# A two-layer hybrid encoder trunk: adding the two scan directions of every head on VectorE

## The reference, cut to what matters

```python
def ssd_chunked(xs, dt, a, bm, cm):
    ...
    a_cs = jnp.cumsum((dt * a).reshape(b, c, t, g, e), axis=2)
    ...
    seg = a_cs[:, :, :, None] - a_cs[:, :, None, :]
    decay = jnp.exp(jnp.where(lower, seg, -jnp.inf))
    cb = jnp.einsum('bclgn,bcsgn->bclsg', Cc, Bc)
    y_diag = jnp.einsum('bclsge,bcsgep->bclgep', cb[..., None] * decay, X)
    ...
# called twice, and both results added: y = y_fwd + y_bwd + d_skip * xs
```

## Time and profile before

| | |
|---|---|
| time, median of 3 runs | 1656.96 us (1655.63 to 1657.75) |
| the profiled execution: time | 1656.37 us |
| its span on the core | 1654.6 us |
| PE busy | 1634.1 us, 99% of the span |
| DVE busy | 993.3 us, 60% |
| POOL busy | 674.2 us, 41% |
| granted TensorE clock | 1.0 of full speed |

### The profile page before, as it was taken

How to read it: one execution, slowest core, us unless ns; L and a number is a source line. 1 busy time by engine, 2 the same in 40 slices (tenths; PEclk the granted TensorE clock), 3 DMA queues, 4 the chain that set the end, 5 groups by cost and what they waited for, 6 DMA issues and landing times.

```text
span 1654.6 us, 20299 instructions
## 1 busy us (share of the span) xinstructions
PE 1634.1 (99%) x7864; PEld 1297.6 (78%) x7864; DVE 993.3 (60%) x1564; ACT 661.9 (40%) x916; POOL 674.2 (41%) x339
## 2 busy tenths in 40 slices
PE   7999999999999999999999999999999999999999
PEld 5777778877878888888877777787878788888887
DVE  4589869787764455522227898798887554554000
ACT  5455552335343333332244555523443433333221
POOL 3332222233445555554443222223244555555443
PEclk9999999999999999999999999999999999999999
DMA  5532135442222222222224221444522223222223
GB/s 170 139 91 74 60 117 146 134 146 94 90 90 99 93 91 100 89 92 96 92 90 127 87 74 62 124 146 130 149 95 90 90 89 100 92 91 98 95 92 109
DMA packets 57375, 170.93 MB, mean 103 GB/s; under 512 B 5984, under 2 KB 11872, under 8 KB 57280
## 3 DMA queue, kind: packets, MB, share of 16 engines
q1 hardware_dynamic: 56896, 168.88, 32.1%
q0 software_dynamic: 384, 0.75, 0.4%
HBM read 166.24 MB, written 3.38 MB: 103 GB/s over the span
## 4 chain that ended last, share of the span: by engine, by line
PE 92%; issue 2%; DVE 2%; POOL 1%; DMA 1%; ACT 1%; SPq 0%; DVEq 0%; POOLq 0%; ACTq 0%
PE banks L1158 27%; PE banks L1160 27%; PE banks L1159 27%; PE banks L1257 2%; PE banks L1236 2%; PE banks L1245 2%; PE banks L1322 1%; PE banks L1309 1%; PE banks L1336 1%; DMA sb_w_raw<-w_out 1%; PE banks L1216 1%; DVE sb_h_lo L809 0%; POOL sb_xc L473 0%; PE banks L1293 0%; DVE sb_squares L822 0%
## 5 line engine op out<-in xcount | busy, mean ns | idle before, releaser
L433 POOL TENSOR_TENSOR sb_w_lo<-sb_w_raw,sb_w_hi 128x1024 fp32r<-128x1024 f32 x200 | 482.4, 2412 | 634.9 <-ACT sb_w_hi L528 634.9
L1158 PE MATMUL banks<-sb_h_hi,sb_w_hi 128*128 128x512 f32 x1344 | 550.9, 410 | 11.3 <-POOL sb_w_lo L433 9.9
L528 ACT ACTIVATE sb_w_hi<-sb_w_raw 128x1024 fp32r<-128x1024 f32 x256 | 270.9, 1058 | 706.9 <-PE banks L1160 691.4
L1160 PE MATMUL banks<-sb_h_hi,sb_w_lo 128*128 128x512 f32 x1344 | 530.9, 395 | 0.0
L1159 PE MATMUL banks<-sb_h_lo,sb_w_hi 128*128 128x512 f32 x1344 | 530.6, 395 | 0.0
L1158 PEld LDWEIGHTS banks<-sb_h_hi,sb_w_hi 128*128 128x128 f32 x1344 | 253.5, 189 | 92.4 <-issue 34.7
L1159 PEld LDWEIGHTS banks<-sb_h_lo,sb_w_hi 128*128 128x128 f32 x1344 | 253.8, 189 | 60.9 <-issue 6.5
L1160 PEld LDWEIGHTS banks<-sb_h_hi,sb_w_lo 128*128 128x128 f32 x1344 | 253.5, 189 | 59.4
L1123 DVE TENSOR_TENSOR banks<-banks,sb_rstd 128x512 f32<-128x512 f32 x88 | 61.5, 699 | 145.3 <-PE banks L1160 135.7
L1160 PE MATMUL banks<-sb_ff_hi,sb_w_lo 128*128 128x512 f32 x352 | 138.9, 395 | 0.0
L1159 PE MATMUL banks<-sb_ff_lo,sb_w_hi 128*128 128x512 f32 x352 | 138.9, 395 | 0.0
(11 more groups left out here) (202 smaller groups left out, 2255.9 us busy)
## 6 DMA issues: line engine op xcount, KB each, us to landing
sb_w_raw<-w_in SPq DMA_DIRECT2D x88, 512.0 KB, 3.4
sb_w_raw<-w_up SPq DMA_DIRECT2D x88, 512.0 KB, 3.3
sb_w_raw<-w_out SPq DMA_DIRECT2D x32, 512.0 KB, 3.3
sb_w_raw<-w_down SPq DMA_DIRECT2D x32, 512.0 KB, 3.3
sb_e<-sum_rows SPq DMA_DIRECT2D x16, 512.0 KB, 6.2
sb_bias_t<-bias_rows SPq DMA_DIRECT2D x16, 448.0 KB, 5.6
sb_exp_cs<-sum_rows SPq DMA_DIRECT2D x32, 192.0 KB
sb_w_raw<-w_down SPq DMA_DIRECT2D x16, 384.0 KB, 3.0
```

The lines of the kernel that those rows point to most:

```text
L433: g.tensor_tensor(WLO[:, n % 2, :], W[:, n % 2, :], WHI[:, n % 2, :].bitcast(F32), ALU.subtract).then_inc(w_lo.handle, 1)
L528: sc.activation(WHI[:, n % 2, :], W[:, n % 2, :], ACT.Copy).then_inc(w_hi.handle, 1)
L1158: mm(out, whi, hhi, start=start, stop=False)
L1160: return mm(out, wlo, hhi, start=False, stop=stop)
```

## The change

It does four things. `seg` becomes one subtraction over both directions and all chunks (128x1024, the columns of AS broadcast along the row) and then one minimum with 80 in place, which waits for the subtraction. `add_directions` moves from POOL to DVE, and is done for every head, behind `low_after`. `within` multiplies the sums of both heads: 8 products instead of 12. And `within` waits for the sums of both heads (`gs_done`), no longer for `g_done`.

```diff
--- before.py
+++ after.py
@@ -276,7 +276,7 @@
     cb_mm, cb_done, xs_done, st_mm, sin_done = sem("cb_mm", 2), sem("cb_done", 4), sem("xs_done", 12), sem("st_mm", 12), sem("sin_done", 8)
     seg_done, e_done, g_done, y_mm = (
         sem(n, SSD_HEADS) for n in ("seg_done", "e_done", "g_done", "y_mm"))
-    gs_done = sem("gs_done", SSD_HEADS // 2)
+    gs_done = sem("gs_done", SSD_HEADS)
     yo_mm, y_read, t_read, z_copied, y_comb = (sem(n, 8) for n in ("yo_mm", "y_read", "t_read", "z_copied", "y_comb"))
     z_done = sem("z_done", 2)
     ff_tap, ff_silu, ff_hi, ff_lo = sem("ff_tap", 2 * FF_T), sem("ff_silu_done", FF_T), sem("ff_hi_done", FF_T), sem("ff_lo_done", FF_T)
@@ -458,11 +458,6 @@
             g.tensor_tensor(SQ[:, j % 2, :].rearrange("p (h e) -> p h e", e=64), XT[:, c, :].rearrange("p (h e) -> p h e", e=64),
                             WS[:, c, col:col + 8].unsqueeze(2).to_broadcast([P, 8, 64]), ALU.mult).then_inc(xs_done.handle, 1)
 
-        def add_directions(h):
-
-            pool.wait_ge(*g_done.at(h + 1))
-            g.tensor_tensor(head_e(h)[:, 0, :], head_e(h)[:, 0, :], head_e(h)[:, 1, :], ALU.add).then_inc(gs_done.handle, 1)
-
         def add_backward(t):
             pool.wait_ge(*y_read.at(t + 1))
             g.tensor_tensor(XC[:, t, 0:SEQ - P], XC[:, t, 0:SEQ - P], T[:, 1, 0:SEQ - P], ALU.add).then_inc(t_read.handle, 1)
@@ -492,8 +487,6 @@
                     if 0 <= s - GROUP_AT[grp] < 3:
                         for j in range(2):
                             scale_states(6 * grp + 2 * (s - GROUP_AT[grp]) + j)
-                if s in WEIGH_AT and WEIGH_AT[s] % 2 == 0:
-                    add_directions(WEIGH_AT[s])
                 if s in PAIR_AT:
                     add_backward(PAIR_AT[s])
                 if s in (16, 17):
@@ -899,16 +892,19 @@
         def seg(h):
             dve.wait_ge(*rows_landed[h % 4].at(16 * (h // 4 + 1)))
 
-            for d in range(2):
-                for c in range(QT):
-                    at = slice(P * c, P * c + P)
-                    ins = v.tensor_scalar(head_e(h)[:, d, at], head_e(h)[:, d, at], AS[:, c, column(d, h):column(d, h) + 1], 80.0,
-                                          ALU.subtract, ALU.min)
-            ins.then_inc(seg_done.handle, 1)
+            e = head_e(h).rearrange("p d (c l) -> p d c l", l=P)
+            cols = AS[:, :, :].rearrange("p c (d n) -> p d c n", n=DIR)[:, :, :, h:h + 1]
+            step(v.tensor_tensor(e, e, cols.to_broadcast([P, 2, QT, P]), ALU.subtract))
+            v.tensor_scalar(head_e(h), head_e(h), 80.0, None, ALU.min).then_inc(seg_done.handle, 1)
 
         def weigh(h):
             dve.wait_ge(*e_done.at(h + 1))
             v.tensor_tensor(head_e(h), head_e(h), CB[:, :, :], ALU.mult).then_inc(g_done.handle, 1)
+
+        def add_directions(h):
+
+            dve.wait_ge(*g_done.at(h + 1))
+            v.tensor_tensor(head_e(h)[:, 0, :], head_e(h)[:, 0, :], head_e(h)[:, 1, :], ALU.add).then_inc(gs_done.handle, 1)
 
         def combine(t):
             dve.wait_ge(*y_mm.at(2 * t + 2))
@@ -1066,6 +1062,8 @@
                 if s in WEIGH_AT:
                     weigh(WEIGH_AT[s])
                 low_after(kind, i)
+                if s in WEIGH_AT:
+                    add_directions(WEIGH_AT[s])
                 if s in PAIR_AT:
                     combine(PAIR_AT[s])
                 if kind == "sc" and i % 3 == 1:
@@ -1310,18 +1308,17 @@
 
         def within(t):
 
-            pe.wait_ge(*gs_done.at(t + 1))
-            pe.wait_ge(*g_done.at(2 * t + 2))
+            pe.wait_ge(*gs_done.at(2 * t + 2))
             if t % 4 == 0:
                 pe.wait_ge(*cb_done.at(2 * (t // 4) + 2))
             if t >= 2:
                 pe.wait_ge(*y_read.at(t - 1))
             for c in range(QT):
-                for h, d in ((2 * t, 0), (2 * t + 1, 0), (2 * t + 1, 1)):
+                for h in (2 * t, 2 * t + 1):
                     half = 64 * (h % 2)
                     ins = mm(BANK[half:half + 64, 6 + t % 2, P * c:P * c + P], XT[:, c, 64 * (h % 8):64 * (h % 8) + 64],
-                             head_e(h)[:, d, P * c:P * c + P], start=d == 0, stop=d == h % 2)
-                    if c == QT - 1 and d == h % 2:
+                             head_e(h)[:, 0, P * c:P * c + P], start=True, stop=True)
+                    if c == QT - 1:
                         ins.then_inc(y_mm.handle, 1)
 
         def from_states(t):
```

## The result

The changed kernel takes 1674.86 us (median of 5 runs, 1671.67 to 1675.93) where the kernel before took 1656.96 (median of 5 as well): 1.0105 times as long, 95% interval 1.0093 to 1.0116. That is 17.9 us slower; 1671 was predicted. Its profiled execution has a span of 1674.2 us, 19.6 more than before.

The account below looks back on a forecast made before the run. PE is busy 99%, but DVE has no slack at each group's last pair and sets the delay. Group 0 5.6 us plus group 1 2.0 make 7.6 a layer, 15.2 on 1657.0: 1672, taken as 1671, range 1653 to 1684.

Parts of the forecast that it names:

- The direction and its mechanism: Last pair of both groups: DVE has no slack against PE, so the kernel gets slower; 7.6 us a layer, chance 0.65.
- 6.5 us later at pair 3: Group 0: sums +4.8, differences +1.8, low part +1.1, collisions gone -2.2, idle used -0.9, new collisions +1.9.
- The prices of sum, subtraction and minimum: On DVE, per head: sum 0.69 us (0.60 from start to start), subtraction 1.22, minimum 0.69.
- the two hold-ups of the sum by POOL's L484: Group 0, slots 8 and 11: a POOL instruction holds up DVE's sum; both collisions 2.5 us, 1.9 taken.
- The 8 products form pairs as in `pv`: PE, `within`: heads alternate in a bank's halves, so a pair costs 1.02 us, not 1.90; 14.1 us for 16 pairs.
- rival A: Whole kernel: PE's saving comes through, 14.1 us less, 1643; with waits half as long, 3.3 and 1.5, still 1663; chance 0.13.
- The waits of PE: PE idle ahead of pairs 0, 2, 3 and 7 by about 2, 4, 3 and 4 us; pairs 1, 4, 5, 6 without.
- the gain of pairs 4 and 5: Group 1: PE gains 2 x 0.9 us there, but slot 21's tile comes some 0.5 later and the gain is gone.
- pair 7 later by 2.9: Group 1: ScalarE's chain 1.0, sums 1.2, difference 0.3, low part 1.1, less 0.7; less 0.9 for the pair: +2.0.
- ScalarE's chain: Group 1, ahead of head 14's weigh: DVE's own delay vanishes in its wait for ScalarE, whose chain starts about 1.0 us later.
- The difference: DVE, `seg`: two long instructions take 1.95 us where eight short ones took 1.66, +0.3 us a head.
- C's dearer terms: Rival C: minimum at 1.22 us (+4.2) or as many more POOL collisions, 1680; both 1686; chance 0.15.

Follow-up runs that it names:

- Experiment 1: Two variants of the changed kernel: without the sums of directions (backward direction missing), 1650.49 us; with 12 products a pair again, the odd head's repeated, 1680.71 us.
- warm: Changed kernel plus three products of constants on PE ahead of the waits of pairs 3 and 7, results overwritten: 1669.97 us.
- sums_alone: Changed kernel with the eight short instructions of before in `seg`; sums on DVE and 8 products stay: 1669.49 us.
- split_sums: Changed kernel with POOL adding even heads, DVE odd ones right behind the weigh, eight short instructions in `seg`, 8 products a pair: 1662.51 us.

## Why the prediction was right

**The direction and its mechanism** held. DVE sets the last pair of each group, and with sums on it sets it later than PE saves. 6.5 us later at pair 3 was predicted, 6.70 and 7.4 measured. The prices of sum, subtraction and minimum are as forecast, and so are the two hold-ups of the sum by POOL's L484 (1.79 at 284.38, 1.75 at 311.22, where 0.69 is usual: 2.2 us, 1.9 taken). The 8 products form pairs as in `pv`: uncollided, 1.10 us from first start to last end. Experiment 1 shows the sum to be the cause; rival A would need it to vanish, and even then 1650 and not 1643 is what comes.

**The waits of PE.** Predicted about 2, 4, 3 and 4 ahead of pairs 0, 2, 3 and 7. Measured in layer 0: 2.07, 1.61, 3.94 and 2.50; in layer 1: 2.07, 3.58, 2.38 and 3.92. Their sum was roughly right (10.1 and 12.0, for 13) and their places vary, since a delay that shows in one pair is not paid again in the next. Pairs 1, 4, 5 and 6 have none, as said, and the tile of slot 21 took the gain of pairs 4 and 5: it waits 2.41 and 2.06 us where it waited 0.84 and 0.97. DVE is busy 61.35 of 64 us in 249 to 313, 96%; it was 94%.

**A term was missing:** what a wait does to TensorE's clock. The sum counted every wait by its length alone. By the trace the fall costs about 2.8 us behind pair 3 of layer 0, 1.5 in layer 1 and 2.1 behind pair 7 there, 6.4 together; with PE kept busy ahead of these pairs (warm), these places gave it all back, and the kernel 4.9.

**A term was too large:** pair 7 later by 2.9; it was 1.73 and 1.23, together 2.8 us less in two layers. The trace shows which part it is. ScalarE's chain was to come 1.0 us later: counted from pair 4, the weigh of head 14 starts 0.22 us later in layer 0 (388.48 and 354.50, for 379.63 and 345.87) and 0.27 sooner in layer 1. What follows it was to cost 1.9 and costs 1.5 in both layers: head 15's long difference took 3.74 instead of 4.52, and that is its whole price, so that the 0.3 beside it was counted too much.

**The difference** was taken at +0.3 a head as a term that adds up. In the changed kernel it is worth that and a little more (5.4 us against sums_alone, part of it clock: PE's lost pulses, counted as (1 - clock) x 4 us over the stretches from 200 us on without those at the program's end, are 5.1 us in sums_alone and 13.6 after). In the kernel before, where the place is less tight, it is worth nothing. So 1671 came near 1675 with the clock left out and pair 7 over-priced, two errors of opposite sign: 15.2 predicted, + 6.4 for the clock, + 1.1 at pair 3, - 2.8 at pair 7, - 0.4 behind pair 7 of layer 0 make 19.5 of the 19.6 us in the trace. The mechanism was right; that the number is this close is in part luck. In the rivals' sums two figures are off without weight: the 3.3 and 1.5 of A are halves of the delays and not of the waits, and both of C's dearer terms add up to 1688, not 1686.

**Open:** why split_sums still loses 6 us. Its PE waits 13.3 us in `within` where the kernel before waits 3.2, and eight DVE sums a layer explain the direction, but no run takes them apart. Open too is what decides whether the clock falls behind a wait (see the last section).

## What to carry to other kernels

Work taken from the busiest engine is worth only what its supplier leaves: here PE did 14 us less and 6 came off even with no sum at all, so look first for the row where the bound engine already waits (0.42 and 1.20 us) and put nothing in front of it on that supplier. Idle time of an engine in a chain of hand-overs (difference, exponential, weigh) wasn't room here. A wait of a few us on TensorE can cost more than its length, and a few useless products ahead of it can buy a part of that back.

## What the runs showed of the hardware

- The granted clock fell behind a wait of 3.94 us (0.55 and 0.60 in the next two stretches) and of 3.92 us (0.50), but not behind one of 2.50 us in layer 0 of the same execution; behind 2.38 us in layer 1 it fell to 0.73 and 0.84. Length alone doesn't decide: behind pair 0's wait of 2.07 us it fell in layer 0 (0.58) and not in layer 1, and in sums_alone it fell behind 3.36 us ahead of pair 2 in layer 0 (0.58) and not behind 3.37 us ahead of the same pair in layer 1. At half clock a product of 128x512 started every 0.43 us instead of 0.23.
- Two instructions that meet, one on DVE and one on POOL, cost 1 us for the one that starts 0.15 us later: 2.24 against 1.22 us for the same low part, 1.30 against 2.21 for the same addition. The Trainium skill, SBUF — State Buffer, section "Who interferes with whom", says that the shared port pair goes to the one that starts first, for the whole instruction, also where a VectorE instruction has both inputs in SBUF and GpSimd reads SBUF, as here. The traces agree: the late one ends about its own usual time behind the end of the other. So a shift of 0.3 us can move a stage by 1 us in either direction, and the price of an edit measured in one surrounding (seg: 0 us) doesn't hold in another (5.4 us).
